# Retention's v of the last 16 tokens: eight products on four column groups of the array, partial sums added on VectorE

## What is computed

```python
q, k, v, g = jnp.split(h @ w_in, SPLIT_RET, axis=-1)
q = _rotary(q.reshape(B, T, RET_HEADS, RET_QK_DIM), cos, sin)
k = _rotary(k.reshape(B, T, RET_HEADS, RET_QK_DIM), cos, sin) * (RET_QK_DIM ** -0.5)
v = v.reshape(B, T, RET_HEADS, RET_V_DIM)
...
qk = jnp.einsum('bhid,bhjd->bhij', qn, kn).astype(F32_2) * decay_intra
o = (jnp.einsum('bhij,bhjv->bhiv', qk, vf) + ...)
...
o = _rms_noaffine(o).reshape(B, T, 2 * D_MODEL).astype(h.dtype)
return (jax.nn.silu(g) * o) @ w_out
```

## Time and profile before

| | |
|---|---|
| median of 3 runs | 2709.34 us |
| the profiled execution | 2710.97 us |
| its span in the trace | 2709.1 us |
| TensorE matmuls busy | 2550.0 us, 94% |
| VectorE busy | 942.8 us, 35% |
| ScalarE busy | 545.7 us, 20% |
| GpSimd busy | 149.3 us, 6% |
| mean granted clock of TensorE | 0.955 of full speed |

### The profile page before, as it was taken

How to read it: one execution, slowest core, us unless ns; L and a number is a source line. 1 busy time by engine, 2 the same in 40 slices (tenths; PEclk the granted TensorE clock), 3 DMA queues, 4 the chain that set the end, 5 groups by cost and what they waited for, 6 DMA issues and landing times.

```text
span 2709.1 us, 31056 instructions
## 1 busy us (share of the span) xinstructions
PE 2550.0 (94%) x11552; PEld 1922.8 (71%) x11552; DVE 942.8 (35%) x1673; ACT 545.7 (20%) x1144; POOL 149.3 (6%) x193
## 2 busy tenths in 40 slices
PE   7999999969999978959899999999999988999999
PEld 3555456658888866836788888756756767888888
DVE  7231266440000014055333552243333243435432
ACT  2300055321111113153111110102112111121100
POOL 1000054201111110000000000000000000000000
PEclk9899989869999989968999999999999999999999
DMA  8201122119888863200132322221211212223221
GB/s 330 98 15 55 52 80 102 47 64 343 329 325 326 330 250 120 71 0 16 55 92 79 86 85 93 96 68 39 93 54 39 85 47 86 81 83 93 81 87 58
DMA packets 83345, 307.12 MB, mean 113 GB/s; under 512 B 9264, under 2 KB 9264, under 8 KB 82624
## 3 DMA queue, kind: packets, MB, share of 16 engines
q1 hardware_dynamic: 75888, 274.24, 29.6%
q0 software_dynamic: 7376, 31.77, 3.0%
HBM read 292.86 MB, written 13.11 MB: 113 GB/s over the span
## 4 chain that ended last, share of the span: by engine, by line
PE 89%; DVE 5%; ACT 3%; issue 2%; DMA 1%; SPq 0%; DVEq 0%; POOL 0%; ACTq 0%; POOLq 0%
PE products L1307 38%; PE products L840 10%; PE products L1188 9%; PE products L994 7%; PE products L1200 4%; PE products L1433 2%; PE products L1045 2%; PE products L1377 1%; PE products L904 1%; PE products L1118 1%; PE products L948 1%; PE products L855 1%; PE products L958 1%; PE products L1058 1%; PE products L1013 1%
## 5 line engine op out<-in xcount | busy, mean ns | idle before, releaser
L1307 PE MATMUL products<-normed,ring 128*128 128x264 f32 (+1 forms) x1312 | 304.8, 389 | 11.3 <-DVE normed L2459 11.3
L1307 PEld LDWEIGHTS products<-normed,ring 128*128 128x128 f32 x1312 | 252.7, 193 | 56.5 <-issue 16.0
L1188 PEld LDWEIGHTS products<-arena,ring 128*128 128x128 f32 x2176 | 248.2, 194 | 8.8 <-issue 8.8
L1529 ACT ACTIVATE arena<-products 128x264 f32<-128x264 f32 (+3 forms) x263 | 118.5, 468 | 666.5 <-PE products L840 201.7
L1188 PE MATMUL products<-arena,ring 128*128 128x128 f32 x2176 | 248.5, 277 | 0.8 <-ACT arena L1677 0.8
L840 PE MATMUL products<-normed,ring 128*128 128x264 f32 (+2 forms) x736 | 219.2, 460 | 3.5 <-DVE normed L1869 3.5
L840 PEld LDWEIGHTS products<-normed,ring 128*128 128x128 f32 x736 | 140.6, 191 | 82.1 <-issue 65.6
L994 PE MATMUL products<-ring,normed 128*128 128x512 f32 (+1 forms) x416 | 182.9, 600 | 8.4 <-DVE normed L1869 8.4
L1307 PE MATMUL products<-arena,mixed 128*128 128x256 f32 (+1 forms) x832 | 189.4, 382 | 0.0
L1307 PEld LDWEIGHTS products<-arena,mixed 128*128 128x128 f32 x832 | 158.1, 190 | 23.8
L1307 PE MATMUL products<-normed,mixed 128*128 128x264 f32 (+1 forms) x704 | 161.5, 382 | 0.0
(11 more groups left out here) (439 smaller groups left out, 3057.5 us busy)
## 6 DMA issues: line engine op xcount, KB each, us to landing
ring<-in_weights SPq DMA_DIRECT2D x303, 512.0 KB, 4.2
ring<-in_experts SPq DMA_DIRECT2D x204, 512.0 KB, 5.0
arena<-results SPq DMA_DIRECT2D x8, 512.0 KB, 7.2
residual<-in_x POOLq DMA_DIRECT2D x1, 2048.0 KB, 15.6
arena<-in_dft_half POOLq DMA_DIRECT2D x1, 2048.0 KB, 8.5
token_rows<-arena SPq DMA_DIRECT2D x4, 512.0 KB, 2.6
out<-residual SPq DMA_DIRECT2D x8, 256.0 KB, 4.5
arena<-in_bias POOLq DMA_DIRECT2D x1, 1920.0 KB, 23.8
```

The source lines that it names most:

```text
L1188: m = pe.matmul(ps[:, side, m_ * P:(m_ + 1) * P], w[:, k, :], job_t[:, k, :], start=(k == 0), stop=(k == KT - 1))
L1307: m = pe.matmul(bank(p, n), left(k), right(k), start=(fresh and k == 0), stop=(k == kt - 1), skip_group_check=True)
L1529: act.activation(out, src, ACT.Copy, scale=scale).then_inc(bank_free[p.bank], 1)
```

## The change

In each turn of TensorE's loop the four groups of 128 tokens stay as they are. For the last 16 tokens the eight products go to four column groups of the array: product k writes to the partitions 32 * (k % 4) and on of the bank, so k = 0 and 4 add up in the partitions 0 to 15, 1 and 5 in 32 to 47, 2 and 6 in 64 to 79, 3 and 7 in 96 to 111. ScalarE's copy of this group is gone. VectorE copies the first partial sum to `ret_v` and adds the three others to it, each instruction waiting for the one before.

```diff
-                    for t, p in enumerate(r["ret", "v"]):
-                        n = P if t < 4 else META
-                        token_major(p, lambda k, t=t, n=n: h2[:, k, t * P:t * P + n], w, n, t == 4, it)
+                    for t, p in enumerate(r["ret", "v"][0:4]):
+                        token_major(p, lambda k, t=t: h2[:, k, t * P:t * P + P], w, P, False, it)
+                    p = r["ret", "v"][4]
+                    fill(p, it)
+                    for k in range(KT):
+
+                        o = 32 * (k % 4)
+                        m = pe.matmul(ps[o:o + META, p.bank, :], h2[:, k, S:T2], w[k // 2][:, k % 2, :], start=(k < 4), stop=(k >= 4),
+                                      skip_group_check=True)
+                        if k % 2 == 0:
+                            begin(m)
+                    finish(p, m)
...
-                    for t, p in enumerate(r["ret", "v"]):
-                        n = P if t < 4 else META
-                        copy(p, ret_v[0:n, t], ps[0:n, p.bank, :], it=it)
+                    for t, p in enumerate(r["ret", "v"][0:4]):
+                        copy(p, ret_v[:, t], bank(p), it=it)
...
-                    me.loop(it, 17)
+                    me.loop(it, 20)
                     two_halves()
                     tile_sums_of(0, it)
                     tile_sums_of(1, it)
+                    p = r["ret", "v"][4]
+                    last = ret_v[0:META, 4]
+                    ready(dve, p, it)
+                    link(dve.tensor_copy(last, ps[0:META, p.bank, :]))
+                    for o in (32, 64):
+                        link(tt_(last, ps[o:o + META, p.bank, :], last, ALU.add))
+                    tt_(last, ps[96:96 + META, p.bank, :], last, ALU.add).then_inc(bank_free[p.bank], 1)
```

## The result

The changed kernel takes 2689.57 us (median of 6 runs, 2685.20 to 2692.81) where the kernel before takes 2709.95 us (6 runs, 2705.47 to 2717.21). The ratio is 0.9922, with a 95% interval of 0.9903 to 0.9941: faster by 0.8%, 20 to 21 us. The forecast was 2689.0 us, in a range of 2684 to 2699.

The account below looks back on a forecast made before the run. TensorE was taken to bound the kernel, its matmuls busy 94% of the span; 5.07 us saved in each of four heads, 20.3 us off 2710.97, then 1.6 for the median, gave 2689.0 us, range 2684 to 2699.

Parts of the forecast that it names:

- TensorE sets the pace of the stage, so its saving comes off the end.: Retention stage: TensorE is on the chain, so 5.07 us saved per head, 20.3 in four, shortens the whole.
- The last group takes 1.9 us.: v's last 16 tokens: from first matmul to q's first product 1.9 us in each head instead of 6.97.
- Column groups run side by side in fp32.: v's last group: four column groups at full rate, four matmuls in a row on each; chance 0.68.
- The estimate from the Trainium skill: v's last group: a speedup of 3.2 for four column tiles, 2.2 us for the group, 19 us saved.
- In order: Rival for v's last group: no matmul passes another, 3.96 us in each head, 2697.3 us in all; chance 0.10.
- two at a time: Case for v's last group: only two column groups overlap, 3.5 us in each head, 2695.5 us; no separate chance given.
- no overlap: Case for v's last group: column groups do not overlap, about 7.0 us in each head, nothing saved; no separate chance given.
- loads in the open: Rival for v's last group: weight loads no longer hidden, 0.527 us a step, 8.4 us per head, 2715.1 us; chance 0.06.
- VectorE's four instructions: 2.9 us, started 0.1 us behind q's first product, 1 us left.: VectorE in each head: copy and three additions take 2.9 us, ending 1 us before q's first addition; no path cost.
- If the cover were gone, the next addition's idle time would take it up.: VectorE in q's products: a late first addition would be absorbed by 4.91 us of idle time before the second.
- The transfers and ScalarE cost nothing.: Retention heads: closer-spaced v tile loads and one 0.59 us ScalarE copy less per head leave the time unchanged.
- The sum against the median.: Whole kernel: profiled 2710.97 us less 20.3 gives 2690.7; the median lies 1.6 us lower, so 2689.0 us.

Follow-up runs that it names:

- the run in pairs: The changed kernel with its eight products reordered, two in a row on the same column group instead of going round the four: 2692.04 us, ratio 0.9926.
- VectorE's part alone: The kernel before, products still on one column group, with ScalarE's copy replaced by four linked VectorE copies of the same piece: 2710.90 us, ratio 0.9994.
- At 16 instructions: The changed kernel with twelve more linked VectorE copies ahead of the additions in each head, in place of four instructions in all: 2698.40 us, ratio 0.9941.

## Why the prediction was right

Point by point, by its own steps:

- *TensorE sets the pace of the stage, so its saving comes off the end.* Right: the head interval fell by 5.14 us for 5.13 us saved in the group.
- *The last group takes 1.9 us.* 1.84 us, the low end of the 1.8 to 1.9 that stood there. Saved 5.13 us in a head where 5.07 was taken: 20.5 us against 20.3 in four heads. From v's first matmul to the end it is 20.7.
- *Column groups run side by side in fp32.* Right, and fuller than the rows of before could show: four at once at the full step of 0.43 us. The reading that carried it was the scores' rows, where a product of another row group had started 0.02 us after one whose second half had still to come; that TensorE passes waiting matmuls is a fact about groups, rows or columns. The estimate from the Trainium skill, "TensorE: Matmul & The Clock Gate", Part 3 (Measured speedup vs the span model), of 2.2 us for the group was too long by 0.36 us.
- *In order, two at a time, no overlap, loads in the open.* 3.96, 3.5, 6.97 and 8.4 us were named for them; 1.84 rules out all four. The run with two groups shows what the second would have looked like (3.54), and was 6.9 us slower than the change by four head intervals (7.6 by the medians) where 6.5 follow from the two forecasts. The Trainium skill, in the same page's Part 3 (The mechanism), has matmuls strictly in order, and loads overlapping matmuls in flight only in another row group. These traces do not agree: the sixteen loads of the group, 0.37 us in all and for the same rows, lie under its matmuls, which are busy for 1.81 of 1.81 us, and in the run in pairs a matmul passes nine others.
- *VectorE's four instructions: 2.9 us, started 0.1 us behind q's first product, 1 us left.* 2.84 us (1795.22 to 1798.06), started 0.19 us behind, 0.93 left. VectorE's part alone costs nothing (0.9994), and with four instructions more than that the time that counts is still the same.
- *If the cover were gone, the next addition's idle time would take it up.* Right up to there, and incomplete: what lies behind is the bank of q's P7, which q's P4 takes next, so that P7's addition has to end by 10.8 us after q's first product. At 16 instructions it was late, and TensorE waited 1.5 us in each head.
- *The transfers and ScalarE cost nothing.* Right: TensorE waited for no tile, and ScalarE's busy time fell by 2.6 us with no effect on the time.
- *The sum against the median.* 2689.0 forecast, 2689.57 measured. That it is so close is partly luck, since the runs spread over 7.6 us.

## What to carry to other kernels

A product with few stationary columns and many moving ones costs the array as much as a full one. If it is a sum over k, put the products on the four 32-column groups and add up the partial sums on an engine with idle time: only the matmuls in a row on one group count, and their order in the program did not matter among these sixteen. Before trusting the idle time, follow it past the first late instruction to the first bank or semaphore that TensorE itself waits for. And a saving on TensorE is worth its full size only where the chain shows TensorE's work without a wait, as here. In the windowed attention, where TensorE takes turns with VectorE and ScalarE, shortening its weighted sum of v gave nothing, and the granted clock was lower with it: compare runs at the same granted clock before deciding what a saving was worth.

## What the runs showed of the hardware that I had not expected

- **TensorE passes nine waiting matmuls.** With two products in a row on each group, the first matmul of all four groups had started within 0.06 us.
- **Four moving streams from the same 128 partitions cost no rate.** Each step was 0.43 us for 512 fp32 columns with one, two and four groups, and 0.11 us for 128.
- **The spread of the runs goes with the clock.** Among 11 runs of the kernel before, the four with the highest mean granted clock, 0.958, took 2705.59 to 2708.25 us, and the one with the lowest, 0.950, took 2721.12. In the changed kernel it is 2685.20 us at 0.958 and 2692.44 at 0.953. That is some 1.5 to 2 us for each 0.001, which is why differences of a few us were read from stretches of the trace at full clock and not from whole times. The stage shown above took 79.29 us at 0.80 and 85.14 at 0.72, with the same instructions.
